# Attention in a hybrid diffusion layer: value products by trios of key tiles, row sums by trios added on GpSimd

## The chip, the core and the metric

The kernel runs on one core of a Trainium2 chip. The metric is the device time of one execution in microseconds (us); lower is better. The core has TensorE (PE in the profile, its weight loads PEld), VectorE (DVE), ScalarE (ACT), GpSimd (POOL) and SyncE (SP), which issues DMAs.

## The reference

One layer of a hybrid backbone on 128 context tokens and 1024 latent tokens of width 1024, all in float32: a joint input projection, three token mixers (mLSTM, HGRN2, attention), gated branch projections, an output projection and a SwiGLU FFN. The change touches the attention of the latent tokens alone: 8 query heads of 64 features, 2 key-value heads, 1152 keys (1024 latent and 128 cached).

```python
def one(qblk):
    s = jnp.einsum('bqkgd,bskd->bkgqs', qblk, k).astype(jnp.float32) * scale
    p = jax.nn.softmax(s, axis=-1).astype(v.dtype)
    return jnp.einsum('bkgqs,bskd->bqkgd', p, v)
```

## The kernel before

`attention` runs between the HGRN2 phase and the phase `tail`, and each of them ends with a barrier of all engines. Its main loop goes over 8 query tiles of 128 rows (`tile(i)`, i from 0 to 7) and, inside, over NT = 9 key tiles of 128 (j). A query tile covers all 8 heads: for each of the 2 key-value heads, 4 query heads stand side by side in 512 columns. Every engine's program is written out in its own function, and semaphores tie them together, so the order of the code is the order on each engine.

For each j, TensorE computes the scores of both key-value heads (`scores`, L2150 and L2151, a high and a low part, into one PSUM bank for each key-value head); ScalarE takes the exponentials into one of five buffers `pt` (L2321); TensorE multiplies them with the values (`values`, L2163: 64 array columns for each key-value head, side by side, so two products run in different columns of the array).

The exponent is taken relative to an estimate of the row's maximum. It is made one query tile ahead: `shift_scores(i + 1, h)` (L2131) computes head h's scores with all keys into PSUM banks 0 to 2, VectorE reduces them (`shift`, L2476), and the next head's shift scores overwrite the same three banks, so they wait for that reduce (`pe.wait_ge(sem["mx"], ...)`). `shifts(i + 1, kv)` (L2041) turns four heads' results for the low part of the scores. There is one such step in each j from 1 on.

Row sums: VectorE adds the buffers of key tiles 0 and 1, 2 and 3, 4 and 5 (`pair_up`, L2516). TensorE multiplies the three pair sums and the three last key tiles with 32 columns of ones (`add`, L2170: 8 products of 32 array columns for each). The reciprocal (`inverted`, L2484) goes over 256 columns, and 8 products with a table (`spread_sums`, L2194) repeat it over the 64 features of each head. `normed` (L2490) multiplies the output with it from PSUM, and SyncE sends the rows out (L1982).

GpSimd has only the query side: an inverse norm (L2018) and the rotary embedding of a query tile (L2025 to L2028) for each tile. In the last query tile there is no next one to prepare; there ScalarE and VectorE split operands for the first branch projection, which starts the next phase's work (`ahead`, L2350, L2353 on ScalarE, L2495, L2499 on VectorE). After the loop TensorE runs three thirds of one branch tile (`branch_tile`, L62), with `spread_sums` of the last tile ahead of the third one.

The lines that set the rhythm of a query tile:

```python
                    if more and 1 <= j < NT - 1:
                        shift_scores(i + 1, j - 1)
                    if j:
                        values(i, j - 1)
                    if j in PAIR_AT:
                        pair_sums(i, PAIR_AT.index(j))
                    if j >= 7:
                        sums(i, j - 1)
```

Of the kernel before, what the change touches and what calls it, by code (L numbers as in the profile page):

```python
# [21 lines left out]
P = 128  # L22
# [1853 lines left out]
def attention(nc, g):  # L1876
# [14 lines left out]
    RING = 5  # L1891
    PAIRS = 3
    PAIR_DONE, P_DONE = (1, 2, 4), (3, 5, 6)
    PAIR_AT = (4, 6, 8)
    LAST = LAT // P - 1
    fill = g.fill
    with Phase(nc, "att") as ph:
# [12 lines left out]
        r1, r2 = ph.sb("r1", [P, NT - 1, KV, HD // 2]), ph.sb("r2", [P, NT - 1, KV, HD // 2])  # L1910
# [5 lines left out]
        qtab = ph.sb("qtab", [P, NT - 1, 4, HD // 2])  # L1916
        q = ph.sb("q", [P, AH, HD])
        qtb = ph.sb("qtb", [P, 4, HD // 2])
# [7 lines left out]
        ones, spread = ph.sb("ones", [P, 32]), ph.sb("spread", [P, G, HD])  # L1926
        rs = ph.sb("rs", [P, KV, P])
# [5 lines left out]
                 "part s1 mx nm ptm pte s2 ex pv sums paired rc spread norm evict yout0 yout1 kv dve mly mlw mlhi b0y1 b0y2 b0w b0yh b0wh b0yl b0wl b0mm b0ev b0out0 b0out1 b0out2 b0out3 b0out4 b0out5 b1lo")  # L1933
# [10 lines left out]
        def _(sp):  # L1944
# [60 lines left out]
        def _(gp):  # L2005
# [6 lines left out]
            gp.wait_ge(sem["qd"], 3)  # L2012
            gp.tensor_tensor(qrs[:], qms[:], khalf[:, 0:AH], ALU.pow).then_inc(sem["qpow"], 1)

            def rope(n):

                gp.wait_ge(sem["qd"], 4 * n + 4 + 3)
                gp.tensor_tensor(qrs[:], qms[:], khalf[:, 0:AH], ALU.pow).then_inc(sem["qpow"], 1)  # L2018
# [3 lines left out]
                w = lambda c: qtb[:, c, :].unsqueeze(1).broadcast_to([P, AH, HD // 2])  # L2022
                for e in range(2):
                    a, b = (0, 1) if e == 0 else (2, 3)
                    gp.tensor_tensor(u1[:], x[:, :, :, 0], w(a), ALU.mult).then_inc(sem["rope"], 1)  # L2025
                    gp.tensor_tensor(u2[:], x[:, :, :, 1], w(b), ALU.mult).then_inc(sem["rope"], 1)
                    gp.wait_ge(sem["rope"], 6 * n + 3 * e + 2)
                    gp.tensor_tensor(o[:, :, :, e], u1[:], u2[:], ALU.subtract if e == 0 else ALU.add).then_inc(sem["rope"], 1)  # L2028
                    gp.wait_ge(sem["rope"], 6 * n + 3 * e + 3)

            for n in range(LAST + 1):
                rope(n)
# [12 lines left out]
        def _(pe):  # L2045
# [89 lines left out]
            def shifts(i, kv):  # L2135
                pe.wait_ge(sem["nm"], AH * i + G * kv + G)
                pe.wait_ge(sem["pte"], turn(i, 2 + kv))
                if kv == 0 and i >= 2:
                    pe.wait_ge(sem["norm"], i - 1)
# [13 lines left out]
            def values(i, j):  # L2153

                n = NT * i + j
                pe.wait_ge(sem["ex"], 2 * n + 2)
                if j == 0:
# [4 lines left out]
                for kv in range(KV):  # L2162
                    mm = pe.matmul(ps[kv * HD:kv * HD + HD, OB, :], va[:, j, kv, 0:HD], pt[n % RING][:, kv, :],  # L2163
                                   start=j == 0, stop=j == NT - 1)
# [9 lines left out]
            def pair_sums(i, p):  # L2174

                u = PAIRS * i + p
                pe.wait_ge(sem["paired"], u + 1)
                if p == 0 and i:
                    pe.wait_ge(sem["rc"], i)
                add(pair[u % 2], p == 0, False)  # L2180

            def sums(i, j):
                add(pt[(NT * i + j) % RING], False, j == NT - 1)

            def spread_sums(i):

                pe.wait_ge(sem["rc"], i + 1)
                if i < LAST:
                    pe.wait_ge(sem["pte"], turn(i + 2, 2) if i + 2 <= LAST else turn(LAST, 3) + 1)
                else:  # L2190
                    pe.wait_ge(sem["norm"], i)
                for a in range(G):
                    for kv in range(KV):
                        mm = pe.matmul(ps[kv * HD:kv * HD + HD, PT, a * P:a * P + P], spread[:, a, :], rs[:, kv, :],  # L2194
                                       start=True, stop=True)
                mm.then_inc(sem["spread"], 1)

            def tile(i):

                more = i < LAST  # L2200
                for j in range(NT):
# [8 lines left out]
                    if more and 1 <= j < NT - 1:  # L2210
# [1644 lines left out]
```

## Time and profile before

| What | Value |
|---|---|
| median of 3 runs | 2375.9 us (2374.77 to 2378.68) |
| the profiled execution | 2374.82 us, its span 2373.0 us |
| mean granted TensorE clock | 0.991 |
| PE busy | 2295.2 us, 97% of the span |
| DVE, ACT, POOL busy | 1426.0 us (60%), 805.5 us (34%), 224.7 us (9%) |
| attention's main loop | scores of its first tile at 1161.81 us, branch tile behind it at 1396.15 us |

The span is the time from the first to the last instruction of one profiled execution; the execution itself took 1.8 us more. "Busy" of PE counts overlapping and waiting products too, so 97% does not mean that the array computes all the time. The starts of one engine's blocks in the timeline are a better measure: from the start of one block to the start of the next.

### The profile page before, as it was taken

How to read it: one execution, taken by the hardware profiler on the slowest of the kernel's cores; microseconds unless marked ns; L12 is line 12 of the kernel's file. 1: busy time of each engine (PE TensorE's matmuls, PEld its weight loads, DVE VectorE, ACT ScalarE, POOL GpSimd, SP SyncE). 2: the span in 40 equal slices, each digit the busy share in tenths (PEclk: the TensorE clock that was granted, in tenths of full speed). 3: DMA queues.
4: the chain of work that ended last, by engine and by line, in shares of the span. 5: the costliest groups of instructions: out<-in, count | busy, mean ns of one | idle time of the engine just before them, and what ended most of it. 6: DMA issues, size and time to landing. Idle time of an engine off the chain costs nothing. (4 is left out here: it accounts for less than half of the span.)

```text
span 2373.0 us, 43700 instructions
## 1 busy us (share of the span) xinstructions
PE 2295.2 (97%) x17959; PEld 2029.6 (86%) x17959; DVE 1426.0 (60%) x2212; ACT 805.5 (34%) x1398; POOL 224.7 (9%) x245
## 2 busy tenths in 40 slices
PE   6999999999999899998899999998999999999997
PEld 5887779999999889998655569877999999998886
DVE  5331266533555467665677646768676676677877
ACT  5321132213333233223344444325223222234444
POOL 0000000001110011112222101000111121120001
PEclk9999999999999999999999999999999999999999
DMA  6324632235452532214101138421222222259434
GB/s 279 120 85 182 225 112 107 100 135 202 155 173 86 198 107 87 83 66 158 44 19 48 56 112 312 154 92 59 79 104 91 76 107 91 73 183 271 129 98 124
DMA packets 126877, 295.60 MB, mean 125 GB/s; under 512 B 19808, under 2 KB 63280, under 8 KB 117376
## 3 DMA queue, kind: packets, MB, share of 16 engines
q1 hardware_dynamic: 98112, 238.67, 29.9%
q10 hardware_dynamic: 24640, 39.46, 4.5%
q0 software_dynamic: 3968, 15.21, 1.7%
q8 instruction: 118, 1.93, 0.3%
q14 instruction: 39, 0.32, 0.0%
HBM read 207.83 MB, written 85.53 MB: 124 GB/s over the span
## 5 line engine op out<-in xcount | busy, mean ns | idle before, releaser
L62 PE MATMUL ps<-prj_w,h_hi 128*128 128x512 f32 (+1 forms) x864 | 254.2, 378 | 4.2 <-DVE h_lo L755 4.2
L62 PE MATMUL ps<-h_hi,fill_whi 128*128 128x384 f32 x672 | 235.8, 351 | 4.7 <-ACT fill_st L1119 2.4
L62 PE MATMUL ps<-h_lo,fill_whi 128*128 128x384 f32 x672 | 226.6, 337 | 3.5 <-issue 3.5
L62 PE MATMUL ps<-wt 128*128 128x320 f32 (+2 forms) x1046 | 227.2, 327 | 2.3 <-DVE merged L3308 1.3
L62 PE MATMUL ps<-h_hi,fill_wlo 128*128 128x384 f32 x672 | 226.5, 337 | 0.0
L62 PE MATMUL ps<-ys,mergedr 128*128 128x256 f32 (+1 forms) x1056 | 219.9, 297 | 0.4 <-issue 0.4
L62 PE MATMUL ps<-zb,mergedr 128*128 128x320 f32 (+2 forms) x764 | 199.8, 326 | 4.9 <-issue 2.7
L62 PE MATMUL ps<-zb,wt 128*128 128x384 f32 (+3 forms) x758 | 200.2, 325 | 0.0
L62 PEld LDWEIGHTS ps<-prj_w,h_hi 128*128 128x128 f32 x864 | 157.3, 190 | 43.0 <-issue 10.6
L62 PEld LDWEIGHTS ps<-wt 128*128 128x128 f32 x1046 | 179.6, 189 | 16.6 <-issue 2.6
L62 PEld LDWEIGHTS ps<-ys,mergedr 128*128 128x128 f32 x1056 | 174.6, 191 | 0.7 <-issue 0.7
L62 PE MATMUL ps<-prj_w,h_lo 128*128 128x512 f32 (+1 forms) x432 | 161.7, 374 | 0.0
L62 PE MATMUL ps<-xb,mergedr 128*128 128x320 f32 (+1 forms) x528 | 156.9, 297 | 0.0
L62 PE MATMUL ps<-ys,wt 128*128 128x384 f32 (+2 forms) x736 | 147.2, 322 | 3.9 <-PEq L82 2.5
L62 PEld LDWEIGHTS ps<-zb,mergedr 128*128 128x128 f32 x764 | 136.6, 190 | 14.9 <-issue 4.6
L62 PEld LDWEIGHTS ps<-zb,wt 128*128 128x128 f32 x758 | 138.9, 189 | 4.6
L1119 ACT ACTIVATE fill_st<-ps 128x384 f32<-128x384 f32 x84 | 41.2, 491 | 281.3 <-PE ps L62 256.7
L62 PEld LDWEIGHTS ps<-h_hi,fill_whi 128*128 128x128 f32 x672 | 127.4, 190 | 7.6 <-ACT fill_st L1119 3.1
L62 PEld LDWEIGHTS ps<-ys,wt 128*128 128x128 f32 x736 | 127.3, 192 | 5.4 <-issue 4.3
L62 PEld LDWEIGHTS ps<-h_hi,fill_wlo 128*128 128x128 f32 x672 | 127.5, 190 | 3.8 <-issue 3.7
L62 PEld LDWEIGHTS ps<-h_lo,fill_whi 128*128 128x128 f32 x672 | 127.7, 190 | 0.0
L2321 ACT ACTIVATE att_pt<-ps 128x512 f32<-128x512 f32 x144 | 78.4, 596 | 110.8 <-PE ps L2151 110.8
(512 smaller groups left out, 4654.1 us busy)
## 6 DMA issues: line engine op xcount, KB each, us to landing
wraw<-in_w_ffn_in SPq DMA_DIRECT2D x22, 1024.0 KB, 5.1
prj_raw<-in_w_ada SPq DMA_DIRECT2D x16, 1024.0 KB, 5.9
fill_raw<-in_w_fill SPq DMA_DIRECT2D x30, 512.0 KB, 4.4
wtf<-a_dram SPq DMA_DIRECT2D x55, 256.0 KB, 2.7
bg_dram<-fill_st ACTq DMA_DIRECT2D x72, 192.0 KB, 2.0
xf<-bg_dram POOLq DMA_DIRECT2D x24, 576.0 KB, 7.4
tok_dram<-prj_tst ACTq DMA_DIRECT2D x45, 256.0 KB, 2.1
prj_raw<-in_w_tok SPq DMA_DIRECT2D x10, 1024.0 KB, 7.3
```

What stands on the lines that cost most here:

```text
L62: mm = pe.matmul(out, lhs[a], rhs[b], start=first and n == 0, stop=last and n == 2, skip_group_check=onto)
L1119: act.activation(self.stage[t], self.g.ps[:, self.bank(u), 0:TH], ACT.Copy).then_inc(self.ev, 1)
L2321: act.activation(pt[n % RING][:, kv, :], ps[:, ST + kv, :], ACT.Exp, scale=QS).then_inc(sem["ex"], 1)
```

## The change

It does the following in the attention loop:

- Values are computed for three key tiles at a time, in j = 3, 6 and 8, in place of one key tile in every j and one at the end.
- VectorE's pair additions and their two buffers are gone. GpSimd adds the three buffers of a trio into the third, by two additions of 128 x 1024 elements, once the values of the trio have read them. The ring has six buffers, and an exponential waits for the GpSimd addition, or for the sums product, that frees its buffer.
- TensorE multiplies one trio sum with 64 columns of ones, 512 columns of data for each key-value head, so the sum stands already repeated over the features; `spread_sums` is gone. The last trio of a query tile is summed in j = 3 of the next one. The last trio of the last tile is summed directly, from its three buffers.
- The reciprocal covers 512 columns, the multiplication with it reads it from SBUF. On VectorE the reciprocal stands behind the shift of head 2, the multiplication behind that of head 3; the query norms and splits are moved, and the copy of the rotary table is gone. SyncE issues a query load ahead of the wait for the output rows.

```diff
@@ def attention
-    RING = 5
-    PAIRS = 3
-    PAIR_DONE, P_DONE = (1, 2, 4), (3, 5, 6)
-    PAIR_AT = (4, 6, 8)
+    RING, TRIO = 6, 3
+    LASTG = (LAT // P) * NT // TRIO - 1
...
-            pair = [over(f"pair{i}", [P, KV, G * P]) for i in range(2)]
...
-        ones, spread = ph.sb("ones", [P, 32]), ph.sb("spread", [P, G, HD])
-        rs = ph.sb("rs", [P, KV, P])
+        ones = ph.sb("ones", [P, HD])
+        rs = ph.sb("rs", [P, G * P])
@@ SyncE, loop over query tiles
+                if i + 5 < NT:
+                    queries_in(i + 5)
                 sp.wait_ge(sem["norm"], i + 1)
                 rows_out(i + 1)
-                if i + 5 < NT:
-                    queries_in(i + 5)
@@ GpSimd
+            def add_trio(n):
+
+                a, b, c = (pt[(TRIO * n + x) % RING] for x in range(TRIO))
+                gp.wait_ge(sem["pv"], n + 1)
+                gp.tensor_tensor(c[:], c[:], a[:], ALU.add).then_inc(sem["paired"], 1)
+                gp.wait_ge(sem["paired"], 2 * n + 1)
+                gp.tensor_tensor(c[:], c[:], b[:], ALU.add).then_inc(sem["paired"], 1)
+
...
-            for n in range(LAST + 1):
-                rope(n)
+            inverse_norm(3)
+            for i in range(LAST + 1):
+                if i:
+                    add_trio(3 * i - 1)
+                if i + 2 <= LAST:
+                    rope(i + 2, 0)
+                add_trio(3 * i)
+                if i + 2 <= LAST:
+                    rope(i + 2, 1)
+                add_trio(3 * i + 1)
+                if i + 3 <= LAST:
+                    inverse_norm(i + 4)
@@ TensorE
+            def values(i, g):
...
+                for j in range(TRIO * g, TRIO * g + TRIO):
+                    n = NT * i + j
+                    pe.wait_ge(sem["ex"], 2 * n + 2)
+                    for kv in range(KV):
+                        mm = pe.matmul(ps[kv * HD:kv * HD + HD, OB, :], va[:, j, kv, 0:HD], pt[n % RING][:, kv, :],
+                                       start=j == 0, stop=j == NT - 1)
                 mm.then_inc(sem["pv"], 1)
 
             def add(x, first, last):
                 for kv in range(KV):
-                    for a in range(G):
-                        mm = pe.matmul(ps[32 * a:32 * a + 32, SB, kv * P:kv * P + P], ones[:], x[:, kv, a * P:a * P + P],
-                                       start=first and kv == 0, stop=last and kv == KV - 1)
+                    mm = pe.matmul(ps[kv * HD:kv * HD + HD, SB, :], ones[:], x[:, kv, :], start=first, stop=last)
+                return mm
+
+            def sums(n):
+
+                i, g = divmod(n, NT // TRIO)
+                if g == 0 and i:
+                    pe.wait_ge(sem["rc"], i)
+                if n < LASTG:
+                    pe.wait_ge(sem["paired"], 2 * n + 2)
+                    mm = add(pt[(TRIO * n + TRIO - 1) % RING], g == 0, g == 2)
+                else:
+                    for x in range(TRIO):
+                        mm = add(pt[(TRIO * n + x) % RING], False, x == TRIO - 1)
                 mm.then_inc(sem["sums"], 1)
...
-                    if i and j == 2:
-                        spread_sums(i - 1)
+                    if more and j >= 1:
+                        shift_scores(i + 1, j - 1)
                     if more and j == 5:
                         shifts(i + 1, 0)
...
-                    if j:
-                        values(i, j - 1)
-                    if j in PAIR_AT:
-                        pair_sums(i, PAIR_AT.index(j))
-                    if j >= 7:
-                        sums(i, j - 1)
-                    if more and j == NT - 2:
-                        shift_scores(i + 1, AH - 1)
+                    if j == 3:
+                        if i:
+                            sums(3 * i - 1)
+                        values(i, 0)
+                    if j == 6:
+                        values(i, 1)
+                        sums(3 * i)
+                    if j == 8:
+                        values(i, 2)
+                        sums(3 * i + 1)
                 if more:
                     shifts(i + 1, 1)
-                values(i, NT - 1)
-                sums(i, NT - 1)
+                else:
+                    sums(LASTG)
@@ ScalarE, exponentials
+                b, r = divmod(n - RING, TRIO)
+                if b >= 0 and r < 2:
+                    act.wait_ge(sem["paired"], 2 * b + r + 1)
+                if b >= 0 and r == 2:
+                    act.wait_ge(sem["sums"], b + 1)
@@ VectorE
             def inverted(i):
-                v.wait_ge(sem["sums"], (NT - PAIRS) * (i + 1))
+                v.wait_ge(sem["sums"], 3 * i + 3)
...
-                v.reciprocal(rs[:].rearrange("p k n -> p (k n)"), ps[:, SB, 0:KV * P]).then_inc(sem["rc"], 1)
+                v.reciprocal(rs[:], ps[:, SB, :]).then_inc(sem["rc"], 1)
...
-                v.tensor_tensor(x, x, ps[:, PT, :], ALU.mult).then_inc(sem["norm"], 1)
+                v.tensor_tensor(x, x, rs[:], ALU.mult).then_inc(sem["norm"], 1)
...
+                if 0 <= i < NT - 3:
+                    norm_b(i + 3)
                 for h in range(AH):
                     if i < LAST:
                         shift(i + 1, h)
-                    if i >= 1 and h == 0:
+                    if i >= 1 and h == 2:
+                        inverted(i - 1)
+                    if i == LAST and h == 5:
+                        ahead()
+                    if i >= 1 and h == 3:
                         normed(i - 1)
...
+                    if 0 <= i < NT - 4 and h == 5:
+                        norm_a(i + 4)
                 if i + 2 <= LAST:
+                    next_split(i + 2, 0)
                     next_split(i + 2, 1)
```

Places in the instruction order. TensorE, in a query tile from j = 3 on, before (L2150 and L2151 are scores, L2131 shift scores, L2163 values, L2170 sums):

```order
L2131 MATMUL ps<-att_kthi,att_qt 128x384 x3
L2163 MATMUL ps<-att_pt,att_va 64x512 x2
L2150 MATMUL ps<-att_qt,att_kthi 128x512
L2151 MATMUL ps<-att_qm,att_ktlo 128x512
L2150 MATMUL ps<-att_qt,att_kthi 128x512
L2151 MATMUL ps<-att_qm,att_ktlo 128x512
L2131 MATMUL ps<-att_kthi,att_qt 128x384 x3
L2163 MATMUL ps<-att_pt,att_va 64x512 x2
L2170 MATMUL ps<-att_pair,att_ones 32x128 x8
```

and now (L2165 and L2166 are scores, L2148 shift scores, L2185 sums, L2179 values):

```order
L2148 MATMUL ps<-att_kthi,att_qt 128x384 x3
L2185 MATMUL ps<-att_pt,att_ones 64x512 x2
L2179 MATMUL ps<-att_pt,att_va 64x512 x6
L2165 MATMUL ps<-att_qt,att_kthi 128x512
L2166 MATMUL ps<-att_qm,att_ktlo 128x512
L2165 MATMUL ps<-att_qt,att_kthi 128x512
L2166 MATMUL ps<-att_qm,att_ktlo 128x512
L2148 MATMUL ps<-att_kthi,att_qt 128x384 x3
L2165 MATMUL ps<-att_qt,att_kthi 128x512
L2166 MATMUL ps<-att_qm,att_ktlo 128x512
L2165 MATMUL ps<-att_qt,att_kthi 128x512
L2166 MATMUL ps<-att_qm,att_ktlo 128x512
```

Between two blocks of shift scores there were four score products and one values block; now there are four score products alone, except where three values blocks stand together.

VectorE, from the reciprocal of one query tile to the multiplication by it, before (L2484 reciprocal, L2476 and L2478 the shift of a head, L2490 the multiplication, L2516 a pair addition):

```order
L2484 RECIPROCAL att_rs<-ps 128x256
L2476 TENSOR_REDUCE att_mx<-ps 128x1
L2478 TENSOR_SCALAR att_qpart<-att_mx 128x1
L2490 TENSOR_TENSOR att_yt<-att_yt,ps 128x512
L2476 TENSOR_REDUCE att_mx<-ps 128x1
L2478 TENSOR_SCALAR att_qpart<-att_mx 128x1
L2516 TENSOR_TENSOR att_pair<-att_pt 128x1024
```

and now (L2479, L2471 and L2473, L2485 in the same roles):

```order
L2479 RECIPROCAL att_rs<-ps 128x512
L2471 TENSOR_REDUCE att_mx<-ps 128x1
L2473 TENSOR_SCALAR att_qpart<-att_mx 128x1
L2485 TENSOR_TENSOR att_yt<-att_yt,att_rs 128x512
L2471 TENSOR_REDUCE att_mx<-ps 128x1
L2473 TENSOR_SCALAR att_qpart<-att_mx 128x1
```

The multiplication now has two operands in SBUF where one was in PSUM, and stands between the shifts of heads 3 and 4 in place of those of heads 0 and 1.

GpSimd, one query tile of the change (L2029 and L2031 are the two additions of a trio, L2019 to L2022 half a rotary embedding, L2010 the inverse norm):

```order
L2029 TENSOR_TENSOR att_pt<-att_pt 128x1024
L2031 TENSOR_TENSOR att_pt<-att_pt 128x1024
L2019 TENSOR_TENSOR att_u<-att_qn,att_qtab 128x256
L2020 TENSOR_TENSOR att_u<-att_qn,att_qtab 128x256
L2022 TENSOR_TENSOR att_qr<-att_u 128x256
L2029 TENSOR_TENSOR att_pt<-att_pt 128x1024
L2031 TENSOR_TENSOR att_pt<-att_pt 128x1024
L2019 TENSOR_TENSOR att_u<-att_qn,att_qtab 128x256
L2020 TENSOR_TENSOR att_u<-att_qn,att_qtab 128x256
L2022 TENSOR_TENSOR att_qr<-att_u 128x256
L2029 TENSOR_TENSOR att_pt<-att_pt 128x1024
L2031 TENSOR_TENSOR att_pt<-att_pt 128x1024
```

The six additions are new; the rest was there before, without the additions between.

## Rows read from the trace of the kernel before

**Rows 1.** Page: the span, and busy time of each engine.

```profile
span 2373.0 us, 43700 instructions
PE 2295.2 (97%) x17959; PEld 2029.6 (86%) x17959; DVE 1426.0 (60%) x2212; ACT 805.5 (34%) x1398; POOL 224.7 (9%) x245
```

**Rows 2.** Timeline, PE, query tile 3: start us, us, operation, xcount [idle before <-releaser].

```profile
1251.70 0.49 PE L2150 MATMUL ps<-att_qt,att_kthi 128*128 128x512 f32 x1
...
1255.31 1.08 PE L2163 MATMUL ps<-att_pt,att_va 128*64 128x512 f32 x4
1256.32 0.49 PE L2150 MATMUL ps<-att_qt,att_kthi 128*128 128x512 f32 x1
...
1257.44 1.09 PE L2194 MATMUL ps<-att_rs,att_spread 128*64 128x128 f32 x16
1258.47 0.79 PE L2131 MATMUL ps<-att_kthi,att_qt 128*128 128x384 f32 x3
...
1260.20 0.49 PE L2150 MATMUL ps<-att_qt,att_kthi 128*128 128x512 f32 x1
...
1261.23 0.68 PE L2131 MATMUL ps<-att_kthi,att_qt 128*128 128x384 f32 x3
1261.84 1.08 PE L2163 MATMUL ps<-att_pt,att_va 128*64 128x512 f32 x4
...
1265.51 0.64 PE L2170 MATMUL ps<-att_pair,att_ones 128*32 128x128 f32 x16
1266.08 0.50 PE L2150 MATMUL ps<-att_qt,att_kthi 128*128 128x512 f32 x1
...
1276.10 0.79 PE L2131 MATMUL ps<-att_kthi,att_qt 128*128 128x384 f32 x3 [0.35 <-DVE att_mx L2476]
1276.72 0.40 PE L2150 MATMUL ps<-att_qt,att_kthi 128*128 128x512 f32 x1
...
1278.77 0.65 PE L2170 MATMUL ps<-att_pair,att_ones 128*32 128x128 f32 x16
...
1279.78 0.65 PE L2041 MATMUL ps<-ident,att_qpart 128*65 128x128 f32 x4
...
1281.95 0.50 PE L2150 MATMUL ps<-att_qt,att_kthi 128*128 128x512 f32 x1
```

**Rows 3.** Timeline, DVE: a reduce behind that waited block; then the reciprocal's group by line.

```profile
1276.92 1.36 DVE L2476 TENSOR_REDUCE att_mx<-ps 128x1 f32<-128x1152 f32 x1 [0.69 <-PE ps L2131]
...
L2484 DVE RECIPROCAL att_rs<-ps 128x256 f32<-128x256 f32 x8 | 14.1, 1757 | 8.0 <-PE ps L2170 8.0
```

**Rows 4.** GpSimd: a rotary product in the loop, 512-column one in the next phase.

```profile
1272.30 0.73 POOL L2028 TENSOR_TENSOR att_qr<-att_u 128x256 f32<-128x256 f32 x1
...
1673.18 1.29 POOL L2909 TENSOR_TENSOR merged<-merged,hole 128x512 f32<-128x512 f32 x1 [50.46 <-DVE hole L3331]
```

**Rows 5.** DVE beside these two, and the 512-column form when GpSimd is idle.

```profile
1272.44 1.67 DVE L2516 TENSOR_TENSOR att_pair<-att_pt 128x1024 f32<-128x1024 f32 x1
...
1673.19 1.82 DVE L3286 TENSOR_TENSOR wt<-zf,wt 128x512 fp32r<-128x512 f32 x1
...
1725.82 0.68 DVE L3286 TENSOR_TENSOR mergedr<-wraw,mergedr 128x512 fp32r<-128x512 f32 x1
```

**Rows 6.** Timeline of the last query tile: its start on PE, ScalarE in it.

```profile
1372.29 0.49 PE L2150 MATMUL ps<-att_qt,att_kthi 128*128 128x512 f32 x1
...
1375.16 1.09 ACT L2321 ACTIVATE att_pt<-ps 128x512 f32<-128x512 f32 x2
1376.11 1.19 ACT L2350 ACTIVATE ys<-ys 128x1152 fp32r<-128x1152 f32 x1
...
1382.92 1.92 ACT L2353 ACTIVATE wt<-wraw 128x2048 fp32r<-128x2048 f32 x1
```

**Rows 7.** Timeline behind the loop: two branch thirds, the last rows' DMA.

```profile
1396.15 4.46 PE L62 MATMUL ps<-ys,wt 128*128 128x384 f32 x24
...
1402.39 0.36 SPq L1982 DMA_DIRECT2D y_dram<-att_yt  x1
```

More of the change, by code:

```diff
@@ L1932, in attention @@
         names = ("load qload const knd kpow kout ktm kte qd qpow rope cpart qtm qte csmm cmx cex cptm cpte comm cdone "
-                 "part s1 mx nm ptm pte s2 ex pv sums paired rc spread norm evict yout0 yout1 kv dve mly mlw mlhi b0y1 b0y2 b0w b0yh b0wh b0yl b0wl b0mm b0ev b0out0 b0out1 b0out2 b0out3 b0out4 b0out5 b1lo")
+                 "part s1 mx nm ptm pte s2 ex pv paired sums rc norm evict yout0 yout1 kv dve mly mlw mlhi b0y1 b0y2 b0w b0yh b0wh b0yl b0wl b0mm b0ev b0out0 b0out1 b0out2 b0out3 b0out4 b0out5 b1lo")
         sem = {n: ph.sem(n) for n in names.split()}
@@ L2021, in rope @@
                 o = qr[:].rearrange("p h (d e) -> p h d e", e=2)
[L2022 to L2032 removed]
+                w = lambda c: qtab[:, n, c, :].unsqueeze(1).broadcast_to([P, AH, HD // 2])
+                a, b = (0, 1) if e == 0 else (2, 3)
+                gp.tensor_tensor(u1[:], x[:, :, :, 0], w(a), ALU.mult).then_inc(sem["rope"], 1)
+                gp.tensor_tensor(u2[:], x[:, :, :, 1], w(b), ALU.mult).then_inc(sem["rope"], 1)
+                gp.wait_ge(sem["rope"], 6 * n + 3 * e + 2)
+                gp.tensor_tensor(o[:, :, :, e], u1[:], u2[:], ALU.subtract if e == 0 else ALU.add).then_inc(sem["rope"], 1)
+                gp.wait_ge(sem["rope"], 6 * n + 3 * e + 3)
+            def add_trio(n):
[4 more added lines that the diff above has]
+                gp.tensor_tensor(c[:], c[:], b[:], ALU.add).then_inc(sem["paired"], 1)
+            inverse_norm(0)
+            for n in range(2):
+                inverse_norm(n + 1)
+                for e in range(2):
+                    rope(n, e)
+            inverse_norm(3)
[10 more added lines that the diff above has]
+                    inverse_norm(i + 4)
         def turn_queries(pe, kv, bank):
@@ L2151, in scores @@
                 pe.matmul(out, kt[1][0:H1, kv, at], qm[i % 2][kv][0:H1, :], start=False, stop=True).then_inc(sem["s2"], 1)
[L2153 to L2157, printed above, removed]
+            def values(i, g):
+                if g == 0:
                     if i:
@@ L2168, in add @@
                 for kv in range(KV):
-                    for a in range(G):
-                        mm = pe.matmul(ps[32 * a:32 * a + 32, SB, kv * P:kv * P + P], ones[:], x[:, kv, a * P:a * P + P],
-                                       start=first and kv == 0, stop=last and kv == KV - 1)
-                mm.then_inc(sem["sums"], 1)
[L2174 to L2196, printed above, removed]
+                    mm = pe.matmul(ps[kv * HD:kv * HD + HD, SB, :], ones[:], x[:, kv, :], start=first, stop=last)
[10 more added lines that the diff above has]
+                        mm = add(pt[(TRIO * n + x) % RING], False, x == TRIO - 1)
+                mm.then_inc(sem["sums"], 1)
             def tile(i):
@@ L2245, in _ @@
             pe.wait_ge(sem["b1lo"], 5)
-            branch_tile(pe, ps, 0, [g.wt[:, 2 * n, :] for n in range(2)], g.ys0, thirds=range(0, 2))
-            spread_sums(LAST)
-            branch_tile(pe, ps, 0, [g.wt[:, 2 * n, :] for n in range(2)], g.ys0, thirds=range(2, 3))
+            branch_tile(pe, ps, 0, [g.wt[:, 2 * n, :] for n in range(2)], g.ys0)
         @block.scalar
@@ L2428, in norm_a, with norm_b @@
                 v.tensor_scalar(qms[:], qss[:], 1.0 / HD, EPS, ALU.mult, ALU.add).then_inc(sem["qd"], 1)
-            def norm_b(n, table):
+            def norm_b(n):
                 v.wait_ge(sem["qpow"], n + 1)
-                if table is not None:
-                    v.tensor_copy(qtb[:], table)
                 v.tensor_tensor(qn[:], q[:], wide(qrs[:], AH), ALU.mult).then_inc(sem["qd"], 1)
@@ L2442, in _ @@
             norm_a(0)
-            norm_b(0, None)
+            norm_b(0)
             v.wait_ge(sem["qd"], 4)
-            v.tensor_copy(spread[:], g.ident[:, 0:P:32].unsqueeze(2).broadcast_to([P, G, HD])).then_inc(sem["dve"], 1)
-            link.n += 1
             for kv in range(KV):
@@ L2506, in next_split @@
                 split(kv, sem["part"])
-            def pair_up(i, p):
-                u = PAIRS * i + p
-                v.wait_ge(sem["ex"], 2 * (NT * i + 2 * p + 2))
-                if u >= 2:
-                    o, op = divmod(u - 2, PAIRS)
-                    v.wait_ge(sem["sums"], (NT - PAIRS) * o + PAIR_DONE[op])
-                a, b = ((NT * i + 2 * p + x) % RING for x in range(2))
-                v.tensor_tensor(pair[u % 2][:], pt[a][:], pt[b][:], ALU.add).then_inc(sem["paired"], 1)
             def tile(i):
-                if i >= 1:
-                    inverted(i - 1)
+                if i == -1:
+                    norm_a(3)
+                if 0 <= i < NT - 3:
+                    norm_b(i + 3)
                 for h in range(AH):
```

44 lines of the change are left out of this document (9 added, 35 removed).

## The prediction

> **What bounds the kernel now.** I read the page first: PE is busy 97% of the span and no other engine over 60% [rows 1], so whatever changes the time of the attention loop has to do it through TensorE, by its work or by its waits. GpSimd is busy 9%: there is room to give it work, and the question is what its work does to others. Then I read the timeline of PE in a middle query tile [rows 2]. There a block's price is the distance from its start to the next block's start. One query tile goes from 1251.70 to 1281.95 us, 30.25 us, and inside it TensorE has one wait for VectorE that can be seen, 0.35 us ahead of the shift scores at 1276.10 [rows 2]. So TensorE's own work sets the pace, and VectorE is just behind it. The loop is 8 such tiles, 1161.81 to 1396.15, 234 us of 2373; no other part of the program changes.
>
> **Prices on TensorE [rows 2].** Values of one key tile: 1255.31 to 1256.32, 1.01 us. One sums visit: 1265.51 to 1266.08, 0.57; two together: 1278.77 to 1279.78, 1.01, so a visit is 0.44 of work and 0.13 of stepping out. `spread_sums`: 1257.44 to 1258.47, 1.03. Two pairs of score products: 1260.20 to 1261.23, 1.03, of which 0.10 is the step in from a narrow visit (shift scores record 0.79 behind one or behind a wait, 0.68 behind scores). Shift scores ahead of a narrow visit 1261.23 to 1261.84, 0.61; behind a wait and ahead of scores 1276.10 to 1276.72, 0.62; so 0.52 between scores, and 0.09 for leaving to narrow columns.
>
> A further key tile of values in the same visit: 16 recorded sums products of 128 columns, four side by side, took 0.44; 4 recorded values products of 512 columns, two side by side, are twice that, 0.87. The new sums product is of the same form (64 array columns, 512 data columns), 0.87 too.
>
> **Work saved.** Before, a tile has nine values visits (9.1), four single sums visits and one double (2.3 + 1.0) and the spread (1.0): 13.4. Now three visits, each of three key tiles and one sum: 4 x 0.87 + 0.14 = 3.6, together 10.9. Ten visits become three: seven times 0.19 for stepping in and leaving is 1.3. TensorE's work falls by 3.8 us in each tile, some 30 us in the loop.
>
> **What the values had covered.** The shift scores of head h + 1 overwrite the banks that VectorE reads for head h. The shortest distance of two such blocks, when TensorE waits, is a ladder of 0.79 for the block [rows 2], 0.04, 1.36 for the reduce [rows 3] and 0.05: 2.24 us (0.04 from the end of the block at 1276.89 to the reduce at 1276.92, as much back). Before, TensorE had scores, shift scores and a values visit in between: 0.93 + 0.10 + 0.61 + 1.01 = 2.65, over the ladder. Now, where no visit lies between, it has 0.93 + 0.52 = 1.45, under it. Four distances are such (heads 0 to 1, 1 to 2, 3 to 4, 6 to 7): 0.8 us of wait each, 3.2. From head 4 to 5 the turn of `shifts` (0.45) lies between too: 0.3. At the tile's start the second pair of scores now waits for ScalarE's copy of the last shifts, which a values visit had covered, and the scores of j = 1 for the exponentials: 0.6, my estimate from ScalarE's 1.09 for two passes over a bank of 512 columns [rows 6]: about one of them stands open. Waits are 4.1 in place of 0.35. So a tile would take 30.25 - 3.8 + 3.75 = 30.2: **the work saved is given back as waits on VectorE's reduces**, almost exactly.
>
> **The reciprocal** doubles to 512 columns, at most 2 x 1.76 = 3.5 us [rows 3]. It starts behind the sums product of j = 3, with the values visit of 2.7 us and the next scores and shift scores (1.8) ahead of the reduce of head 3: hidden, with 0.8 us left.
>
> **GpSimd.** One addition of 128 x 1024 is in no row. The rotary product takes 0.73 for 256 columns, the addition in the next phase 1.29 for 512 [rows 4]: 0.56 for 256 more, so 1.29 + 2 x 0.56 = 2.4 for 1024. From both sides: 2.3 by VectorE's ratio (1.29 to 0.68 for 512 columns [rows 4, 5], applied to 1.23, which is 1.67 less the 0.44 of the block below), 2.9 by four times 0.73. I take 2.4, since the 512-column row is the nearest. A trio is 4.9 us with the wait between; a tile has 3 x 4.9, six rotary products (4.4) and an inverse norm of 8 columns, under one addition: some 21 us of 30. GpSimd is not the bound, and the trios are ready 2 us or more ahead of their sums products, except in the last tile.
>
> **But the two engines block each other.** At 1673.19 VectorE's product of two SBUF operands takes 1.82 us beside GpSimd's of 1.29 that began 0.02 before; with GpSimd idle the form takes 0.68 [rows 4, 5]. It waited 1.14 us, until about 0.15 before GpSimd's end. At 1272.44 a pair addition waited in the same way behind a product that began at 1272.30 [rows 4, 5]. Reduces read PSUM and show 1.36 with or without GpSimd. [...]
>
> The place where it falls on the path is `normed`, now with two SBUF operands and between the shifts of heads 3 and 4. Let V be the end of the first values visit. GpSimd's two additions run from V to V + 2.5 and to V + 4.9, VectorE free of them from V + 4.8. TensorE goes on with scores (1.03) and shift scores of head 3 (0.7 to their end), VectorE's reduce ends 1.4 later, its small product 0.1: `normed` is ready at V + 3.2, in the middle of the second addition. It waits 1.6, runs 0.7, and the reduce of head 4 starts at V + 5.5 in place of V + 4.0. Head 5's shift scores wait for it, and the second values visit behind them: **1.5 us in each tile** with a predecessor and a successor, i = 1 to 6. Such a tile takes 31.6. The other two-operand products of VectorE (norms, splits) lie beside long visits.
>
> **The last tile** has no shift scores, but ScalarE has the `ahead` copies, 1.19 (four) and 1.92 (two) us, one behind each of the first six pairs of exponentials of 1.09 [rows 6]. A step can't be shorter than 2.3 or 3.0 there. Before, a values visit lay in each step; from 1372.29 to 1396.15 the tile took 23.9 [rows 6, 7]. Now TensorE has 1.03 in a step and waits: 0.6 at the start, three times 1.2, 2.0 behind the first long copy (the second lies beside a visit), 0.4 in the last step, and 1.0 for the last pooled trio, which VectorE's `ahead` products delay: 7.6. Its work falls by 1.1 only, since three buffers are summed directly (2.6), and some 0.5 of waits of before goes: 23.9 - 1.1 - 0.5 + 7.6 = 29.9. **6 us more.** Behind the loop `normed` no longer waits for two branch thirds: the last DMA came 6.2 us behind the loop [rows 7], now about 5.0: 1.2 less.
>
> **The sum** against the profiled execution, 2374.8: first tile, without sums or multiplication, -0.4; six tiles at +1.35, +8.1; last tile +6.0; end -1.2: **+12.5, 2387.3**. That execution lies 1.1 under the median, 2375.9; I forecast 2388. SyncE's query load, ahead of its wait for the output rows, and the dropped copy of the rotary table lie beside TensorE's work and count nothing; the load only comes earlier.
>
> **Rivals.**
> [...]
> *GpSimd becomes the bound or nearly*: with 2.9 for an addition a tile has 24 us of GpSimd, `normed` is freed at V + 5.8, one microsecond later in six tiles, and the last tile's additions and VectorE's `ahead` products, which exclude each other, add 4 to 6: 2398. For it: 0.73 for 256 columns, taken four times, gives it [rows 4], and blocks that VectorE lays on GpSimd come on top. Against: the 512-column row.
> *The work saved stays saved*: **faster**. If the ladder were shorter than the 1.45 of work between its rungs, only the work would count: -3.8 in eight tiles, 2346. It decides at a reduce of 0.57 us, and the row has 1.36 [rows 3]; a partial form, visits a microsecond cheaper than I think, gives 2365.
> *The change does not do what it says* (the values are not run in one visit): the order shows six products together, so no chance of its own.
>
> **How the numbers follow.** A measurement of this kernel tells 0.2%, about 4.8 us, from no change. Forecast 0.62; GpSimd heavier 0.18; no block 0.14, on either side of +4.8; saved 0.06. Range: from 2378, below the case without a block, to 2400, above the heavy additions; it leaves out the fast case and tails. Faster 0.06, same 0.11, slower 0.83.
>
> **What would show it.** In the profile of the changed kernel: values and sums in three blocks of 3.6 us; shift scores without a visit between at 2.2 to 2.3 us, with waits for `att_mx`; GpSimd's additions at 2.4 us; `normed` recorded at over 2 us; tiles of 31 to 32 us, the last of 30. A tile under 30 would refute the ladder; a `normed` of 0.7 would refute the block; waits of the sums products on GpSimd in middle tiles would show the heavy case.

## The result, and the profile after

| | before | after |
|---|---|---|
| median, same chip | 2375.3 us (2373.3 to 2378.7, 4 runs) | 2397.6 us (2393.5 to 2402.9, 4 runs) |
| ratio | | 1.0093 [1.0076, 1.0111]: slower |
| profiled execution, its span | 2374.8, 2373.0 | 2402.9, 2401.1 |
| first tile, start to start | 29.4 | 28.9 |
| tile i = 1 | 30.3 | 32.5 |
| tiles i = 2 to 6 | 29.8 to 30.3 | 34.1 to 34.5 |
| last tile | 23.9 | 33.6 |

The time lies inside the range and on the forecast side, 10 us above the forecast of 2388. The profiled execution of after is the longest of its four and by itself lies above the range of 2400; its 28.1 us of span difference are more than the 22.3 of the medians. They add up as: -2.7 ahead of the loop (1.5 of it where a half-clock stretch of before, at 536.8, is absent), -0.4 in the first tile, +2.2 in tile 1, +20.1 in the five tiles behind it, +9.7 in the last, -2.3 behind the loop, +1.6 in the rest (the parts are rounded).

The head of the page of after, to be read against [rows 1]:

```profile
span 2401.1 us, 42106 instructions
PE 2289.7 (95%) x17167; PEld 2014.9 (84%) x17167; DVE 1448.4 (60%) x2179; ACT 804.0 (33%) x1398; POOL 338.9 (14%) x291
```

TensorE is no longer busy for 97% but for 95%: work has gone and idle time has come. The timeline of PE in the tile from 1220.45 to 1254.58, which answers to [rows 2] (start, duration, then in brackets the idle time ahead and who ended it; L2165 and L2166 are scores, L2148 shift scores, L2179 values, L2185 sums, L2053 and L2058 the turns, that is the transpositions on TensorE, of queries and shifts):

```profile
1224.59 0.63 PE L2053 MATMUL ps<-ident,att_qpart 128*128 128x128 f32 x4 [0.98 <-DVE att_qpart L2437]
1224.97 0.77 PE L2148 MATMUL ps<-att_kthi,att_qt 128*128 128x384 f32 x3
...
1227.19 0.80 PE L2148 MATMUL ps<-att_kthi,att_qt 128*128 128x384 f32 x3 [0.51 <-DVE att_mx L2471]
...
1229.44 0.79 PE L2148 MATMUL ps<-att_kthi,att_qt 128*128 128x384 f32 x3 [0.50 <-DVE att_mx L2471]
1230.15 1.08 PE L2185 MATMUL ps<-att_pt,att_ones 128*64 128x512 f32 x4
1231.06 2.75 PE L2179 MATMUL ps<-att_pt,att_va 128*64 128x512 f32 x12
...
1234.79 0.69 PE L2148 MATMUL ps<-att_kthi,att_qt 128*128 128x384 f32 x3
...
1237.02 0.76 PE L2148 MATMUL ps<-att_kthi,att_qt 128*128 128x384 f32 x3 [0.58 <-DVE att_mx L2471]
...
1240.69 0.80 PE L2148 MATMUL ps<-att_kthi,att_qt 128*128 128x384 f32 x3 [1.52 <-DVE att_mx L2471]
1241.41 4.49 PE L2179 MATMUL ps<-att_pt,att_va 128*64 128x512 f32 x12
```

The rungs of the ladder (the distances of two shift-scores blocks with only scores between), 1224.97 to 1227.19 to 1229.44 and 1234.79 to 1237.02, are 2.22 to 2.25 us, as forecast (2.24); a fourth, from 1247.74, is 2.14. The first visit, sums and values, takes 3.59 from its start at 1230.15 to the next scores (forecast 3.6). One wait is much longer, 1.52 ahead of the shift scores of head 5 at 1240.69. And two things are in no step of the prediction: a wait of 0.98 at the tile's start, and a second values visit of 4.49 us for the same 12 products that take 2.75 in the first.

The timelines of DVE and then of POOL in the same tile, which answer to [rows 3 to 5]:

```profile
1220.80 1.05 DVE L2436 CAST att_qpart<-att_qr 128x256 fp32r<-128x256 f32 x1 [2.01 <-PE ps L2058]
1221.89 2.55 DVE L2437 TENSOR_TENSOR att_qpart<-att_qr,att_qpart 128x256 fp32r<-128x256 f32 x1
...
1231.73 3.36 DVE L2479 RECIPROCAL att_rs<-ps 128x512 f32<-128x512 f32 x1
...
1236.99 2.38 DVE L2485 TENSOR_TENSOR att_yt<-att_yt,att_rs 128x512 f32<-128x512 f32 x1
1239.29 1.34 DVE L2471 TENSOR_REDUCE att_mx<-ps 128x1 f32<-128x1152 f32 x1
...
1252.17 0.29 DVE L2436 CAST att_qpart<-att_qr 128x256 fp32r<-128x256 f32 x1
1252.50 0.43 DVE L2437 TENSOR_TENSOR att_qpart<-att_qr,att_qpart 128x256 fp32r<-128x256 f32 x1
```

```profile
1219.35 2.36 POOL L2029 TENSOR_TENSOR att_pt<-att_pt 128x1024 f32<-128x1024 f32 x1 [0.97 <-PE ps L2179]
1221.78 2.38 POOL L2031 TENSOR_TENSOR att_pt<-att_pt 128x1024 f32<-128x1024 f32 x1
...
1233.97 2.39 POOL L2029 TENSOR_TENSOR att_pt<-att_pt 128x1024 f32<-128x1024 f32 x1 [6.59 <-PE ps L2179]
1236.43 2.38 POOL L2031 TENSOR_TENSOR att_pt<-att_pt 128x1024 f32<-128x1024 f32 x1
```

`normed` (L2485) starts at 1236.99, inside the addition of 1236.43, and lasts 2.38 in place of 0.69; the reduce behind it starts at 1239.29, 5.55 us behind the end of the first values visit (forecast 5.5). The same block stands at the tile's start: the split product L2437 takes 2.55 beside an addition and 0.43 without one at 1252.50. It is what the queries' turn at 1224.59 waits for.

The granted clock of three stretches of after (the tile, its slow values and sums visits, the last tile; columns: window, its length, PE busy and records, granted clock, DMA share, GB/s):

```profile
1220.45:1254.58 34.13, 29.24 (x127) 0.95 0.06 16
1241.41:1246.69 5.28, 5.28 (x17) 0.68 0.01 3
1391.36:1424.93 33.57, 29.18 (x100) 0.85 0.03 9
```

and of the two tiles of before:

```profile
1251.70:1281.95 30.25, 29.90 (x229) 1.00 0.07 18
1372.29:1396.15 23.86, 23.57 (x189) 1.00 0.04 12
```

A stretch recorded at a granted clock of 1.00 is called full clock here, one at 0.50 half clock. In the tiles 2 to 6 of after one stretch of 3.4 us at 0.50 lies in each tile, from 1241.8 in the one shown, 1.1 us behind the end of the long wait; there it lies in the second values visit, whose 4.49 us are 1.7 more than the 2.75 of the first, half of the 3.4. In the last tile it is two stretches, 10.2 us. Before has none in the whole loop, 1161.81 to 1396.15 (granted 1.00).

That is one execution. The four of after took 2393.5, 2395.3, 2399.9 and 2402.9 us at mean granted clocks of 0.991, 0.990, 0.988 and 0.985, and the last of them is the one profiled, with 70 us at 0.50 in all. From these means, as an estimate, the shortest had about 29 us less at half clock, about as much as the 27.2 that lie in the loop here. Where they lay no trace shows, but most of the loop's stretches were probably not in that execution, and the median holds only a part of what they cost in the profiled one.

### The profile page after: what moved, and what is told of

Read it like the earlier page. It is cut to its first block and busy times, and to the rows that moved or that the text cites. A ratio compares the mean times of both kernels' runs of the same rounds, so it can differ in the third digit from the quotient of the medians.

```text
span 2401.1 us, 42106 instructions
## 1 busy us (share of the span) xinstructions
PE 2289.7 (95%) x17167; PEld 2014.9 (84%) x17167; DVE 1448.4 (60%) x2179; ACT 804.0 (33%) x1398; POOL 338.9 (14%) x291
## 5 line engine op out<-in xcount | busy, mean ns | idle before, releaser
L2471 DVE TENSOR_REDUCE att_mx<-ps 128x1 f32<-128x1152 f32 x64 | 86.8, 1356 | 62.1 <-PE ps L2148 62.1
```

The costliest lines, as they stand in the source:

```text
L2471: v.tensor_reduce(mx[:, a % 2:a % 2 + 1], ps[:, 0:3, 0:TH], AX.XY, ALU.max).then_inc(sem["mx"], 1)
```

## The experiments

All times are medians, each ratio, as recorded, is to the kernel before on the same chip. The kernel before had medians of 2374.5, 2375.1 and 2375.8 us in the three groups of runs, and dividing the medians gives up to 0.1% more than the ratios shown. Tile lengths are distances of the first score product of one tile to that of the next.

**GpSimd's additions almost empty.** Leaves most of the row sums out: an addition covers 8 of the 512 columns of each key-value head.

```diff
-                gp.tensor_tensor(c[:], c[:], a[:], ALU.add)
+                gp.tensor_tensor(c[:, :, 0:8], c[:, :, 0:8], a[:, :, 0:8], ALU.add)
```

(the second addition likewise)

> GpSimd's two additions of a trio cover 8 of the 512 columns of each key-value head, so the row sums are left incomplete; all else is as in the changed kernel (2397.6 us, middle tiles of 34.1 us). Theory (ladder of shift scores, plus blocks of VectorE by GpSimd's additions, plus half-clock stretches behind those waits): the multiplication drops from 2.4 to 0.7 us, the blocked split from 2.6 to 0.4, the half-clock stretches inside the middle tiles vanish, tiles fall to 30.0 to 30.5, the whole to 2374 to 2382; the ladder's waits of 0.6 to 0.7 us stay. Rival (the tiles are longer by TensorE's own work or by the ladder alone, the blocks lie beside it): tiles stay at 33 or more and the whole at 2390 or more.

Measured: 2377.8 us (2375.8 to 2383.3, 10 runs), ratio 1.0007 [0.9997, 1.0017]. Middle tiles 29.8, a little under the 30.0 to 30.5 that I had given, last tile 32.7. `normed`, as a group of DVE in this kernel and then in after (least, median and greatest ns):

```profile
L2485 DVE TENSOR_TENSOR att_yt<-att_yt,att_rs x7: 691/691/693, 1206.7 to 1383.6; 128x512 f32<-128x512 f32 x7
```

```profile
L2485 DVE TENSOR_TENSOR att_yt<-att_yt,att_rs x6: 2316/2396/2678, 1204.5 to 1373.8; 128x512 f32<-128x512 f32 x6
```

With the additions small, the middle tiles lose 4.3 us and have no half-clock stretch. So everything that the middle tiles cost over before comes with the additions' length, and the ladder without blocks gives 29.8, 0.4 below the 30.2 of the prediction. The last tile keeps 8.9 of its 9.7: it is another matter.

**`normed` out of the additions.** One line of VectorE's order is changed, and in the last tile `ahead` is moved behind head 6.

```diff
-                    if i >= 1 and h == 3:
+                    if i >= 1 and h == 5:
                         normed(i - 1)
```

> The multiplication by the reciprocal moved from behind the shift of head 3 to behind that of head 5, where GpSimd is idle; nothing left out. Theory: the block of 1.6 us on the path goes, and with it the half-clock stretch behind it, 1.5 + 1.7 us in each of five or six tiles: tiles of 31 to 32, the whole 2378 to 2388; the blocked split at the tile's start stays. Rival (the clock falls for the general lack of work and not behind this wait): only 1.5 in each tile, tiles of 32.5, the whole 2388 to 2391. Rival two (the block lies beside other waits): no change, 2397.

Measured: 2387.1 (2384.9 to 2389.0, 4 runs), ratio 1.0043 [1.0027, 1.0060]. `normed` takes 0.69, middle tiles 30.98, and the granted clock in them is 1.00:

```profile
1220.00:1251.00 31.00, 27.56 (x126) 1.00 0.06 18
```

Tile 1 of after, which has no half-clock stretch, takes 32.45: the block at `normed` is 32.45 - 30.98 = 1.5 us a tile. The other 1.7 of the 34.15 went with the half clock in the profiled executions of the two kernels. The blocked split stays (CAST 1.05, product 2.55), and 30.98 is 1.2 over the 29.8 of the kernel with small additions: that is the price of the block at the tile's start.

**Both blocks away.** As above, and GpSimd starts the trio 3i - 1 behind VectorE's splits and query norm in place of ahead of them (tiles up to i = 5).

```diff
                 if i:
+                    if i + 3 <= 8:
+                        gp.wait_ge(sem["qd"], 4 * (i + 3) + 4)
                     add_trio(3 * i - 1)
```

> The kernel with the late multiplication (2387.1 us, middle tiles of 31.0), and GpSimd's additions of the trio that ends a query tile wait for VectorE's query norm, so that they no longer meet the split of the next query tile. Theory (the split's 1.05 and 2.55 us, blocked, make the second turn of the queries late by 1.1 us in each tile): both fall to 0.3 and 0.4, the wait goes, tiles of 29.8 to 30.0, the whole 2379 to 2382. Rival (the turn is late for another reason, or the sums product in j = 3 now waits for GpSimd): no gain, 2386 or more.

Measured: 2379.8 (2375.8 to 2383.1, 10 runs), ratio 1.0017 [1.0008, 1.0027]. Tiles up to i = 5 take 29.8, tile 6, which the added wait does not cover, 30.98. Here are tiles 5 and 6:

```profile
1311.37:1341.17 29.80, 27.36 (x127) 1.00 0.16 64
1341.17:1372.15 30.98, 27.55 (x127) 1.00 0.03 9
```

The two differ by the block at the tile's start, 1.2, in one and the same run. With whole additions the tiles are now as short as with empty ones. The kernel is still slower, by its last tile of 33.8.

**The ladder made longer.** VectorE reduces 384 columns more ahead of each head's reduce.

```diff
+                v.tensor_reduce(mxc[:, h:h + 1], ps[:, 0:1, 0:TH], AX.XY, ALU.max)
                 v.tensor_reduce(mx[:, a % 2:a % 2 + 1], ps[:, 0:3, 0:TH], AX.XY, ALU.max).then_inc(sem["mx"], 1)
```

> The changed kernel with a second, shorter reduce (384 of the 1152 columns, about 0.5 us, its result not used) ahead of each head's reduce on VectorE. Theory: the ladder becomes 0.5 us longer at each of four or five distances in a tile, so tiles of the middle gain 2.0 to 2.7 us, 12 to 18 us in all over the changed kernel's 2397.6: 2409 to 2416. Rival (VectorE's reduces are not on the path; it is idle 40% of the time): within 4 us of 2397.6.

Measured: 2414.7 (2409.5 to 2417.6, 4 runs), ratio 1.0165 [1.0148, 1.0182]. From PE's timeline:

```profile
1233.79 0.78 PE L2148 MATMUL ps<-att_kthi,att_qt 128*128 128x384 f32 x3
...
1236.48 0.80 PE L2148 MATMUL ps<-att_kthi,att_qt 128*128 128x384 f32 x3 [0.97 <-DVE att_mx L2472]
...
1239.20 0.79 PE L2148 MATMUL ps<-att_kthi,att_qt 128*128 128x384 f32 x3 [0.97 <-DVE att_mx L2472]
```

Each rung grew from 2.24 to 2.70 and each wait from 0.50 to 0.97, by the 0.47 that the added reduce takes until the next may start. So what VectorE needs longer goes into the rungs one for one, and the rival is refuted. The profiled tiles fit this only at equal clock. Tiles 1 to 6 take 34.2 to 34.6, little over those of after; there is no half-clock stretch in them here, although the waits are longer. Against the 32.45 of a full-clock tile of after it is 1.8 more, where I had given 2.0 to 2.7. The stretch stands in the first tile instead, which takes 34.2 in place of 28.9 (below, the first tile and tile 1):

```profile
1160.77:1194.98 34.21, 29.51 (x123) 0.90 0.05 14
1194.98:1229.27 34.29, 27.53 (x127) 1.00 0.06 16
```

This execution is the shortest of its four (mean clock 0.990; the others have 0.987 and 0.988), that of after the longest, so the loops of the two profiles differ by 7 us and the medians by 17. The rungs explain some 13 of the 17, an estimate from 1.8 in each of seven tiles; that the rest is the clock fits the means, but no trace shows it.

**The waits of the middle tiles filled.** Two or three unused score products of 512 columns go into the PT bank (the PSUM bank of the turns, idle then) ahead of five shift scores of a tile; what they write is not read.

```diff
+                    if more and j in (2, 3, 5, 6, 8):
+                        pe.wait_ge(sem["pte"], turn(i + 1, 1 if j < 6 else 2) + 1)
+                        for x in range(3 if j == 6 else 2):
+                            pe.matmul(ps[:, PT, :], kt[0][:, 0, 0:P], qt[i % 2][0][:], start=True, stop=True)
```

> The changed kernel (2397.6 us; half-clock stretches in five middle tiles) with two or three products of 512 columns more, 0.43 to 0.65 us, whose result is not used, ahead of each of the five shift-scores blocks of a tile that wait for VectorE; their time lies inside those waits. Theory (the granted clock falls there because TensorE waits): no half-clock stretch in the middle tiles, tiles of 32.4 to 32.6 in place of 34.1, the whole 2389 to 2392. Rival (it falls for something else, such as the narrow products): the stretches stay, 2397 or more.

Measured: 2395.8 (2393.7 to 2403.1, 4 runs), ratio 1.0083 [1.0067, 1.0098], hardly less than after and over the 2389 to 2392 that I had given. The tiles of the profiled execution say more than the sum:

```profile
1225.47:1257.92 32.45, 30.15 (x138) 1.00 0.06 17
1257.92:1290.37 32.45, 29.84 (x135) 1.00 0.06 17
```

More work, and the middle tiles are 1.7 us shorter than in after: there is no half-clock stretch in them, and what is left is what the blocks alone make, 32.45. This agrees with the 1.7 that tile 1 of after gave. It does not show by itself that the filling took the stretches away: one execution of each kernel was traced, and the shortest executions of the two kernels are alike, 2393.5 without the filling and 2393.7 with it, both at a mean clock of 0.991. The last tile, which was not filled, took 37.7 in place of 33.6, with VectorE's and GpSimd's products meeting otherwise in it (a wait of 2.6 for the last trio, in place of 1.0) and half clock in three stretches, and gave 4.1 of the gain back; the profiled span, with 4.7 us more ahead of the loop, is after's.

**The last tile alone, by two edits,** both on the kernel with both blocks away (2379.8, last tile 33.8). The first puts the values of the last tile back into one visit for each key tile:

```diff
+                    if not more and j:
+                        values(i, j - 1, 1)
+                    if more and j in (3, 6, 8):
+                        values(i, (0, 3, 6)[(3, 6, 8).index(j)], TRIO)
```

> The kernel of e5_late_gate (middle tiles 29.8 us, last tile 33.8, 2379.8 us), with the value products of the last tile alone in one visit for each key tile, as in e6. Theory 'covered ladder': ScalarE's copies make steps of 2.1 to 2.8 us, and single visits of 1.0 us fill them as they did before the change; the last tile falls to about 26 us, without half-clock stretches inside it, and the time to 2371 to 2374. Rival 'the blocked additions': the last tile is set by GpSimd's and VectorE's products that exclude each other (8.83 us for two, 4.29 for an addition), wherever the visits lie: the last tile stays at 31 to 34 and the time at 2377 to 2381.

Measured: 2373.7 (2371.4 to 2376.8, 12 runs), ratio 0.9993 [0.9984, 1.0001]; last tile 26.5, no half clock in it. The second leaves the visits of three and fills the waits with 17 unused products:

```diff
+                    if not more and j in (1, 2, 3, 6):
+                        unused((0, 1, 3, 4, 0, 0, 5)[j])
...
+                    unused(4)
                     sums(LASTG)
```

> The kernel of e5_late_gate with 17 unused products of 512 columns in the waits of the last tile (1 ahead of the scores of j = 1, 3, 4 and 5 ahead of those of j = 2, 3 and 6, and 4 ahead of the last sums). Theory 'half clock': the half-clock stretches in the last tile (10.2 us of it) follow the waits and cost 3 to 3.5 us; with the waits filled they go, the last tile takes 30 to 31 us as the ladder alone gives, and the time is 2376 to 2377. Rival 'steps of ScalarE and the blocked additions': the tile is set by other engines at whatever clock; it stays at 33 to 35 us, and the time at 2379 to 2382.

Measured: 2376.4 (2373.0 to 2379.4, 12 runs), ratio 1.0002 [0.9993, 1.0011]. Its last tile, and that of the kernel without the filling:

```profile
1368.57:1398.98 30.41, 28.63 (x116) 1.00 0.03 9
```

```profile
1372.15:1405.92 33.77, 29.11 (x99) 0.85 0.03 8
```

With the waits filled the tile takes 30.4 at full clock, and 3.4 us go with the half clock. Here the other executions say the same: the twelve with the filling have mean clocks of 0.991 to 0.993, the ten without it 0.988 to 0.991, and the medians differ by 3.4 us, too. The rival, that the blocked additions set the last tile's length at any clock, is refuted in both: VectorE's first four `ahead` products take 9.5 us in each of them, all six 16.2 with the filling as without it, and the tile is 30.4 and 26.5. A wait for the last trio stays in each (0.9 and 0.4 us, 1.0 without either edit).

**One values visit for each key tile, the rest of the change kept.** This separates the two halves of the change: the visits and the sums on GpSimd.

```diff
-                for j in range(TRIO * g, TRIO * g + TRIO):
...
+                    if j:
+                        values(i, j - 1)
```

> Values of one key tile in each j, as before the change, with all the rest of the change kept (trio sums on GpSimd, 64 columns of ones, no spread). Theory: a visit in each j covers the ladder again, and TensorE keeps the saving of the sums and of the spread, about 1 + 0.2 for the spread and some 0.7 for the sums' steps: tiles of 28.5 to 29.5 if the multiplication's block is covered too, no half clock, last tile back near 24; the whole 2358 to 2370. Rival (the narrow visits' steps were the larger cost, so nine visits cost 6 x 0.33 = 2 us more in each tile than three): 2400 or more.

Measured: 2377.6 (2373.3 to 2383.5, 10 runs), ratio 1.0014 [1.0003, 1.0025]: a miss, over the range that I had given. Tiles 1 to 4 took 30.9, and DVE's timeline shows why (between heads 6 and 7):

```profile
1271.24 2.59 DVE L2421 TENSOR_TENSOR att_q<-att_q 128x512 f32<-128x512 f32 x1
1273.87 0.69 DVE L2423 TENSOR_REDUCE att_qss<-att_q 128x8 f32<-128x512 f32 x1
1274.59 1.50 DVE L2425 TENSOR_SCALAR att_qms<-att_qss 128x8 f32<-128x8 f32 x1
```

`norm_a` now falls on GpSimd's additions, from 1270.91 to 1276.07: its square takes 2.59 in place of 0.68, and even a TENSOR_SCALAR of 8 columns 1.50 in place of 0.17. Shift scores wait 2.0 us behind it. The last tile took 26.0, where I had given near 24. In the two tiles without a `norm_a`, 5 and 6, a tile took 28.6.

**The same with `norm_a` behind head 4,** where GpSimd runs no addition, and a second kernel that has the added GpSimd wait of above too.

```diff
-                    if 0 <= i < NT - 4 and h == 5:
+                    if 0 <= i < NT - 4 and h == 4:
                         norm_a(i + 4)
```

> The kernel with values of one key tile in each j (2377.6 us; tiles of 30.9, of 28.6 without a query norm in them), with the first part of the query norm moved from behind the shift of head 5 to behind that of head 4, away from GpSimd's additions. Theory: the 2.1 us that head 7's shift scores waited behind the blocked norm go, tiles of 28.4 to 28.9, 8 us less in four tiles: 2367 to 2371. Rival (the norm is blocked in the new place as long, or its delay hits head 5's shift scores instead): 2375 or more.

> As the last one, and GpSimd's additions of the trio that ends a query tile wait for VectorE's query norm at the tile's start. Theory: with a values visit behind the last turn the split has time before the additions anyway, so little changes: within 3 us of the last one; slower if the sums product of j = 3 now waits for the additions, which then end some 8.5 us into the tile, against 8.9 when it is due. Rival (the split is on the path here too): 5 to 7 us faster than the last one.

Measured: 2365.7 (2361.8 to 2367.5, 5 runs), ratio 0.9959 [0.9945, 0.9972], just under the range that I had given, and 2364.6 (2361.6 to 2366.9, 5 runs), ratio 0.9957 [0.9943, 0.9971]. Both beat the kernel before by 10 us, and the added wait brings nothing that shows. Middle tiles are 28.6 in both, 1.65 under before, with one wait over 0.5 us left, at the reciprocal, and no half clock in the loop. Tile 2 of the first:

```profile
1213.73:1242.34 28.61, 28.04 (x127) 1.00 0.06 19
```

The last tile is 26.0.

## Why the prediction was right, and where it was off

- *Direction and mechanism.* "The work saved is given back as waits on VectorE's reduces" holds: the rungs measure 2.22 to 2.25 (2.24), and grow one for one with the reduce. Without blocks and half clock a middle tile takes 29.8 (30.2). Against 30.26 of before, the 3.8 us that the prediction counts as saved bring 0.5.
- *The block at `normed`*: 2.38 us for the product (forecast 0.7 + 1.6), 1.5 a tile by experiment (1.5). The product was ready 3.25 us behind the first values visit (3.2). The case without a block (chance 0.14) falls.
- *GpSimd's addition*: 2.38 (2.4); reciprocal 3.36 (at most 3.5), hidden; no sums product of a middle tile waits for GpSimd, so the heavy case falls too, although its time was nearest to the measured one. The range's upper end held the result for a reason that the text did not have: that the median lies inside it is in part luck.
- *First tile* -0.4 (-0.4). *Behind the loop* -2.3 (-1.2): the wait ahead of the next branch products fell from 2.53 to 1.46, and `spread_sums` of the last tile, 1.03, which stood there, was not in the sum.
- **The first step that failed** is the sentence "The other two-operand products of VectorE (norms, splits) lie beside long visits". The split of the second key-value head stands at the tile's start, right behind the trio that the change puts there, and the queries' turn waits for it: 1.2 us in each middle tile, forecast 0. What [rows 5] show was applied at one place and not to each two-operand product in turn; with GpSimd adding in 14 of 34 us of a tile, a product without a planned gap is likely to meet one. Less the 0.4 that the ladder was overrated by, a full-clock tile is 32.45 and not 31.6, 5 us in six tiles.
- **The second is a term that was not in the sum**: the clock. The tiles were priced at a granted clock of 1.00 throughout, which is what the loop of before has. In the profiled execution the half clock took 1.7 us in five tiles and 3.4 in the last, 12 of its 28, more than the split; with the waits filled by unused products neither is there (34.1 to 32.45, and 33.8 to 30.4, each at a granted clock of 1.00). In the median execution it is less, 4 to 7 us: an estimate, since the median lies 4.1 us above the shortest execution and 5.3 under the profiled one (12 - 5.3 is 6.7). At full clock the last tile is 30.4 in the kernel with both blocks away, where 29.9 was forecast; the waits that the 29.9 is made of were not measured one by one at that clock.

The middle tile of the profiled execution as the runs take it apart: 30.26 of before, -0.5 for the work saved less the ladder's waits, +1.2 split, +1.5 `normed`, +1.7 half clock, together 34.2; 34.15 was measured.

## What to carry to other kernels

Work taken off the busiest engine is a gain only where nothing else used it as cover (here 3.8 us a tile brought 0.5): before merging visits, write down the shortest distance that the other engine allows between two blocks, and see whether what remains between them is longer. Where GpSimd is given SBUF additions, lay every VectorE product of that loop beside them on one time line, one-input ones too; moving one line of the order was worth 10 us here, and 12 in the kernel with nine visits. And waits that open in a loop that TensorE had filled can cost twice, once as idle time and once in the granted clock behind them (3.4 us in the last tile here); the second part differs from execution to execution (mean clocks of 0.985 to 0.991 in the four of after), so look at every run's mean clock and not at one profile.

## What had not been expected of the hardware

- Two one-input VectorE instructions on SBUF were held up beside GpSimd's two-input additions as well: the CAST of 128 x 256 took 1.05 us in place of 0.29 (its 1220.80 lies in the addition of 1219.35), the TENSOR_SCALAR of 128 x 8 1.50 in place of 0.17 (its 1274.59 lies in the addition that ends at 1276.07). Reduces from PSUM kept 1.34 to 1.36, and the one reduce from SBUF in the lines of the nine-visit kernel, at 1273.87 inside an addition, its 0.69. The prediction had looked at two-input products alone. Without an addition beside it the CAST of 256 columns is done in 0.29 us, a two-input product of as many in 0.43; why one one-input instruction is held up and another is not, no run shows.
- The half-clock stretches do not simply follow the sum of the waits. The profiled execution of after has one in each of five middle tiles, 1.1 us behind a wait of 1.52 that itself stands behind three of 0.5 to 0.6; that of the kernel with longer rungs waits more, 5.4 us for VectorE's maxima in a tile where after waits 3.6, and has none in those tiles, but one of 6.8 us in its first. What decides it is not settled by these runs. That filling the waits keeps the clock up is borne out for the last tile by the traces (granted 0.85 without the filling, 1.00 with it) and by the medians of all executions (3.4 us apart), for the middle tiles by one trace of each kernel alone (0.95 and 1.00). No wait for a DMA stands in the tile shown; its waits of up to 1.52 us are for VectorE and ScalarE, and it has 0.95 granted.
